# One start stage for the first block: load, norm and transpose by tiles of tokens, rotation table and first weights moved

## The chip, the cores and the metric

The kernel runs on one core of one Trainium2 chip. The metric is the time of one execution on the device in microseconds (us), smaller is better. The kernel is one launch of 42,208 instructions on five engines: TensorE (PE, matrix products; PEld is its weight load), VectorE (DVE), ScalarE (ACT), GpSimd (POOL) and SyncE (SP), which here issues nearly all DMAs. Each engine runs its own list of instructions in order. They meet at semaphores, and at a barrier of all engines at the end of each stage.

## The reference, cut to what matters

The program is two transformer-like blocks over 512 tokens of width 1024, all in float32. The change touches only the head of the first block: the load of `x`, the RMS norm, the transposed copy of the normed tokens, the cosine and sine tables for the rotation, and the beginning of the differential attention.

```python
y = xf * lax.rsqrt(jnp.mean(xf * xf, axis=-1, keepdims=True) + eps)
return (y * w.astype(jnp.float32)).astype(x.dtype)            # rms_norm, eps 1e-6
...
ang = positions.astype(jnp.float32)[..., None] * inv_freq
return jnp.cos(ang), jnp.sin(ang)                             # rotary_tables
...
return jnp.concatenate([t1 * c - t2 * sn, t2 * c + t1 * sn], axis=-1)   # apply_rotary on q and k
...
weights = probs[:, :, 0] - lam * probs[:, :, 1]               # diff_attention, lam from four vectors of 64
```

After the first block's attention come a state space scan, a mixture of 64 experts, two layers of a second block and a last norm. None of these is changed.

## The kernel before, in words

Every part is a stage: a function with the decorator `stage`, which ends with a barrier over all engines, so that the next stage's first instruction comes after the last of the stage before. Within a stage each engine has a hand-written list.

The start of the program is four stages. `stage_load` loads the table of constants (737.5 KB) and all of `x` (2048 KB) with two DMAs and waits for both. `stage_rope_tables` loads the positions, broadcast to 128 partitions, and makes two angle tables of 128x512 on VectorE (`RopeTable.angles`, lines 325 to 347): a cast and a multiplication by the frequencies, then for the cosine and for the sine a reduction of the angle to one turn. ScalarE then takes the two sines (`RopeTable.sines`). The position table lives in the buffer of the cosine, the table of turns in that of the sine. `stage_norm` squares the four tiles of 128 tokens on ScalarE (L401), takes one mean, one root (L405) and one reciprocal for all four, scales the rows on VectorE (L420), transposes them on TensorE in 8 groups of four 128x128 squares (L436), and splits each group into a rounded high part (ACT, L409, `h_hi`) and a remainder (DVE, L424, `h_lo`). All products with weights are made of three products of such parts.

`stage_attention` is a software pipeline over steps `u` from -7 to 35. Its weights are a `Stream` of tiles of 512 KB with three buffers each: SyncE loads a raw tile, ScalarE makes its high part (`make_hi`, L226), VectorE its low part (`make_lo`, L235), and TensorE may then start 24 matmuls with it (L284 to L286, `rows_of`). Each head has three tiles, for q, k and v, cut into four pieces of six rows of three matmuls. ScalarE takes a finished product to SBUF (`evacuate`, L604), TensorE turns its halves by a constant matrix (`half_turn`, L553), and VectorE multiplies by the cosine (L712) and the sine (L714) and adds (L718, in the function `rope`). The second `half_turn` waits until VectorE has read the first one's bank (`aux_roped`). Before the loop VectorE waits for five small DMAs, the four lambda vectors and a column of weights, before it makes the first low part:

```python
v.wait_ge(small_loaded, 80)
v.tensor_tensor(lam_prod[:], lam_rows[:, 0::2, :], lam_rows[:, 1::2, :], ALU.mult)
...
W.make_lo(v, 0)
W.make_lo(v, 1)
v.wait_ge(lam_exp, 1)
```

ScalarE makes two high parts, waits for VectorE's `dots_ready`, takes the exponentials of the lambdas, and enters the loop.

Of the kernel before, what the change touches and what calls it, by code (L numbers as in the profile page):

```python
# [291 lines left out]

@stage
def stage_load(k, x):
    nc = k.nc
    loaded = k.sem("start_loaded")
    with nc.Block() as block:
        @block.sync  # L300
        def _(sp):
            sp.dma_start(k.consts[:], k.const_dram[:, 0:FIRST_COLS]).then_inc(loaded, 16)
            sp.dma_start(k.x[:], x[0].rearrange("(t p) d -> p t d", p=P)).then_inc(loaded, 16)
            sp.wait_ge(loaded, 32)


class RopeTable:

    def __init__(self, k, ctx, tag, positions, freq, cos_out, sin_out):
        self.k, self.positions, self.freq, self.cos, self.sin = k, positions, freq, cos_out, sin_out  # L310
        self.pos_i = k.sb(f"{tag}_pos_i", [P, T], I32, ctx)
        self.pos_f, self.turns = cos_out, sin_out
        self.ang = k.sb(f"{tag}_ang", [P, 2, T], F32, ctx)
        self.pos_loaded, self.ang_ready = k.sem(f"{tag}_pos_loaded"), k.sem(f"{tag}_ang_ready")

    def load(self, sp):

# [1 line left out]

    def angles(self, v):  # L320

        two_pi = 2 * np.pi
# [5 lines left out]
        v.wait_ge(self.pos_loaded, 16)  # L328
        v.tensor_copy(pos[:], self.pos_i[:])
        v.drain()  # L330
        v.tensor_scalar(pos[:], pos[:], self.k.c(self.freq), None, ALU.mult)
        v.drain()
        for n, quarter in ((0, 0.25), (1, 0.0)):
# [15 lines left out]
    def sines(self, a):  # L349

        a.wait_ge(self.ang_ready, 2)
# [5 lines left out]
def stage_rope_tables(k, *table):  # L357

    with ExitStack() as ctx:
        rope = RopeTable(k, ctx, *table)  # L360
        with k.nc.Block() as block:
            @block.sync
            def _(sp):
                rope.load(sp)

            @block.vector
            def _(v):
                rope.angles(v)

            @block.scalar  # L370
            def _(a):
                rope.sines(a)


@stage
# [69 lines left out]


@stage
def stage_attention(k, W, lams, subln_w, att, merged, sig):

    nc = k.nc  # L450
    HEADS, UNITS, LEAD = 8, 32, 7
# [3 lines left out]
    with ExitStack() as ctx:  # L455
# [25 lines left out]
        with nc.Block() as block:  # L481
# [114 lines left out]
            def _(a):  # L596
# [64 lines left out]

                W.make_hi(a, 0)
                W.make_hi(a, 1)
                a.wait_ge(dots_ready, 1)
                a.activation(lam_dots[:], lam_dots[:], ACT.Exp).then_inc(lam_exp, 1)
                for u in range(FIRST, LAST):
                    if u + LEAD < UNITS + KD:
                        piece_before(u + LEAD)
                    if is_unit(u):
                        take_weights(u)  # L670
                    if is_unit(u + 2):
                        exps(u + 2)
                    if is_unit(u - 1):
                        take_out(u - 1)
                    if head_at(u, 5) is not None:
                        root(head_at(u, 5))
                    if head_at(u, 7) is not None:
                        out_hi(head_at(u, 7))
                    piece_after(u + LEAD)
                for m in range(KD):  # L680
                    W.make_hi(a, VALUES + 2 + m)

            @block.vector
            def _(v):
# [24 lines left out]
                def rope(n):  # L709
# [25 lines left out]
                def piece(g):  # L735
# [4 lines left out]
                    if part != 1:  # L740
                        W.make_lo(v, 3 * i + 2 + max(part - 1, 0))
                    if part >= 2:
                        rope(3 * i + part - 2)
# [9 lines left out]
                v.drain()  # L753
                v.tensor_scalar(lam_neg[:], lam_neg[:], -LAM_INIT, None, ALU.add)
                v.drain()
                for u in range(FIRST, LAST):
                    if is_unit(u + 2):
                        mask_and_max(u + 2)
# [7 lines left out]
                        out_lo(head_at(u, 7))  # L766
                    if u + LEAD < UNITS + KD:
                        piece(u + LEAD)
                for m in range(KD):
                    W.make_lo(v, VALUES + 2 + m)  # L770
                    v.wait_ge(W.used, VALUES + m + 1)
# [2730 lines left out]
def first_block(k, ap):  # L3502
# [4 lines left out]
    with ExitStack() as ctx:  # L3507
# [4 lines left out]
        with ExitStack() as h_ctx:  # L3512
            k.make_room_for_h("x", h_ctx, "right")
            with ExitStack() as att_ctx:
                k.make_room_for_rope("1", att_ctx)
                stage_rope_tables(k, "r1", ap["positions"], "freq64", k.cos, k.sin)
                stage_norm(k, "n1", ap["norm_mix_w"][0])
                stage_attention(k, W, [ap[n] for n in ("lambda_q1", "lambda_k1", "lambda_q2", "lambda_k2")], ap["subln_w"][0], k.x, merged, sig)
# [47 lines left out]
def build(nc, ap, consts, out):  # L3566
    with ExitStack() as ctx:
        k = Core(nc, ctx, consts)
        stage_load(k, ap["x"])
# [28 lines left out]
```

## Time and profile before

| | |
|---|---|
| median of 3 runs | 3816.51 us (3810.84 to 3816.89) |
| profiled execution | 3816.76 us, of which the span from first to last instruction is 3814.9 us |
| mean granted TensorE clock in the profiled execution | 0.923 of full speed |
| busy share of the span | PE 86%, PEld 61%, DVE 38%, ACT 29%, POOL 7% |
| first matmul of the attention stage | 54.05 us after the span's start |
| attention stage's first instruction | 42.15 us |

Busy time counts the work that an engine does. A timeline row says when an instruction starts, how long it runs, and how long the engine was idle before it and what ended that idle time. The table of slices gives the granted clock of TensorE, 1.00 for 2.4 GHz and 0.50 for 1.2 GHz.

### The profile page before, as it was taken

How to read it: one execution, taken by the hardware profiler on the slowest of the kernel's cores; microseconds unless marked ns; L12 is line 12 of the kernel's file. 1: busy time of each engine (PE TensorE's matmuls, PEld its weight loads, DVE VectorE, ACT ScalarE, POOL GpSimd, SP SyncE). 2: the span in 40 equal slices, each digit the busy share in tenths (PEclk: the TensorE clock that was granted, in tenths of full speed). 3: DMA queues.
4: the chain of work that ended last, by engine and by line, in shares of the span. 5: the costliest groups of instructions: out<-in, count | busy, mean ns of one | idle time of the engine just before them, and what ended most of it. 6: DMA issues, size and time to landing. Idle time of an engine off the chain costs nothing. (4 is left out here: it accounts for less than half of the span.)

```text
span 3814.9 us, 42208 instructions
## 1 busy us (share of the span) xinstructions
PE 3270.0 (86%) x16302; PEld 2316.5 (61%) x16302; DVE 1443.0 (38%) x2418; ACT 1111.4 (29%) x1899; POOL 269.3 (7%) x272
## 2 busy tenths in 40 slices
PE   4998999989588877887774978889998988969997
PEld 3776778778433333333333846768886846858886
DVE  4772466653420000000103555443323556353332
ACT  3672566652100000000002243232222244232221
POOL 0000222210000000000000001300000000400000
PEclk9999999999799999999996985989999986989999
DMA  3223222223599999999984200033323300023332
GB/s 95 61 67 64 78 56 67 67 62 116 217 417 426 426 426 425 423 422 412 418 339 136 66 12 4 1 94 95 98 96 85 83 12 4 1 78 94 97 97 77
DMA packets 355527, 601.99 MB, mean 158 GB/s; under 512 B 72288, under 2 KB 306560, under 8 KB 330624
## 3 DMA queue, kind: packets, MB, share of 16 engines
q1 hardware_dynamic: 346112, 590.85, 42.4%
q0 software_dynamic: 9216, 8.42, 0.7%
q8 instruction: 133, 2.18, 0.2%
q14 instruction: 66, 0.54, 0.0%
HBM read 603.40 MB, written 20.97 MB: 164 GB/s over the span
## 5 line engine op out<-in xcount | busy, mean ns | idle before, releaser
L1729 PE MATMUL ex_up<-ex_W,ex_XT 128*64 128x512 f32 x1024 | 256.9, 659 | 87.4 <-DMA ex_W<-in_w_expert_up_dram 87.4
L226 ACT ACTIVATE f_hi<-f_raw 128x1024 fp32r<-128x1024 f32 x148 | 156.8, 1059 | 565.6 <-PE ff_bk L286 550.0
L1729 PE MATMUL ex_gp<-ex_W,ex_XT 128*64 128x512 f32 x1024 | 246.4, 636 | 61.8 <-DMA ex_W<-in_w_expert_gate_dram 60.4
L235 DVE TENSOR_TENSOR f_lo<-f_raw,f_hi 128x1024 fp32r<-128x1024 f32 x148 | 181.1, 1224 | 257.4 <-ACT f_hi L226 257.2
L284 PE MATMUL ff_bk<-h_a_hi,f_hi 128*128 128x512 f32 x704 | 275.9, 392 | 2.8 <-DVE h_a_lo L3457 2.8
L285 PE MATMUL ff_bk<-h_a_lo,f_hi 128*128 128x512 f32 x704 | 275.4, 391 | 0.0
L286 PE MATMUL ff_bk<-h_a_hi,f_lo 128*128 128x512 f32 x704 | 275.3, 391 | 0.0
L1758 PE MATMUL ex_yp<-ex_W,ex_hT 128*64 128x512 f32 x1024 | 226.8, 594 | 37.0 <-DMA ex_W<-in_w_expert_down_dram 22.2
L1772 DVE TENSOR_TENSOR ex_hid<-ex_sg,ex_up 128x512 f32<-128x512 f32 x32 | 22.0, 688 | 610.7 <-PE ex_up L1729 610.7
L1729 PEld LDWEIGHTS ex_up<-ex_W,ex_XT 128*64 128x64 f32 x1024 | 93.0, 150 | 250.7 <-issue 250.7
L1729 PEld LDWEIGHTS ex_gp<-ex_W,ex_XT 128*64 128x64 f32 x1024 | 88.7, 146 | 218.6 <-issue 216.8
L235 DVE TENSOR_TENSOR b_lo<-b_raw,b_hi 128x1024 fp32r<-128x1024 f32 (+1 forms) x121 | 147.9, 1234 | 124.4 <-ACT b_hi L226 124.1
L284 PE MATMUL ff_bk<-f_hi,fT_hi 128*128 128x512 f32 x480 | 187.8, 391 | 0.0
L285 PE MATMUL ff_bk<-f_lo,fT_hi 128*128 128x512 f32 x480 | 187.5, 391 | 0.0
L286 PE MATMUL ff_bk<-f_hi,fT_lo 128*128 128x512 f32 x480 | 187.3, 390 | 0.0
L1758 PEld LDWEIGHTS ex_yp<-ex_W,ex_hT 128*64 128x64 f32 x1024 | 84.5, 137 | 157.2 <-issue 157.2
L284 PE MATMUL ss_acc<-h_x_hi,b_hi 128*128 128x512 f32 x320 | 132.6, 414 | 29.6 <-DVE b_lo L235 29.6
L226 ACT ACTIVATE b_hi<-b_raw 128x1024 fp32r<-128x1024 f32 (+1 forms) x121 | 125.7, 1048 | 110.0 <-PE mg_bk L286 64.9
L284 PEld LDWEIGHTS ff_bk<-h_a_hi,f_hi 128*128 128x128 f32 x704 | 133.2, 189 | 31.5 <-DVE h_a_lo L3457 3.6
L286 PEld LDWEIGHTS ff_bk<-h_a_hi,f_lo 128*128 128x128 f32 x704 | 133.1, 189 | 27.8
L285 PEld LDWEIGHTS ff_bk<-h_a_lo,f_hi 128*128 128x128 f32 x704 | 133.2, 189 | 27.5
L286 PE MATMUL ss_acc<-h_x_hi,b_lo 128*128 128x512 f32 x320 | 130.0, 406 | 0.0
(599 smaller groups left out, 6543.9 us busy)
## 6 DMA issues: line engine op xcount, KB each, us to landing
ex_W<-in_w_expert_gate_dram SPq DMA_DIRECT2D x64, 2048.0 KB, 28.8
ex_W<-in_w_expert_up_dram SPq DMA_DIRECT2D x64, 2048.0 KB, 29.1
ex_W<-in_w_expert_down_dram SPq DMA_DIRECT2D x64, 2048.0 KB, 28.9
b_raw<-in_w_in_dram SPq DMA_DIRECT2D x88, 512.0 KB, 3.9
f_raw<-in_w_gate_up_dram SPq DMA_DIRECT2D x88, 512.0 KB, 3.9
f_raw<-in_w_down_dram SPq DMA_DIRECT2D x44, 512.0 KB, 3.5
m_raw<-in_w_in_dram SPq DMA_DIRECT2D x40, 512.0 KB, 4.0
b_raw<-in_w_branch_ssd_dram SPq DMA_DIRECT2D x16, 512.0 KB, 4.0
```

Source lines behind the costliest of these rows:

```text
L226: a.activation(self.hi[n % self.SLOTS][:, at], self.raw[n % self.RAW][:, at], ACT.Copy).then_inc(self.cast, 1)
L235: v.tensor_tensor(self.lo[i][:, at], self.raw[n % self.RAW][:, at], self.hi[i][:, at].bitcast(F32), ALU.subtract).then_inc(self.split_done, 1)
L284: pe.matmul(out, a[0], b[0], start=first, stop=False)
L285: pe.matmul(out, a[0], b[1], start=False, stop=False)
L286: return pe.matmul(out, a[1], b[0], start=False, stop=last)
L1729: ins = pe.matmul(ps[part[e], :], XT[b][:, q, part[e]], row_view(slots[e], KD)[:, q, :], start=(q == 0), stop=(q == KD - 1))
L1758: ins = pe.matmul(y_ps[s][part[e], :], hT[:, q, part[e]], row_view(slots[e], HT)[:, q, s * 512:(s + 1) * 512], start=(q == 0), stop=(q == ...
L1772: v.tensor_tensor(hid[:], sg[:], u_ps[:], ALU.mult).then_inc(hid_ready, 1)
```

## The change

The load of `x`, the norm and the transposes become one stage, `stage_start`. SyncE loads the positions, tile 0 of `x`, the constants, the norm's weights, tiles 1 to 3 of `x` and then the first three tiles of the weight stream. Squares, means, roots, scaling, transposes and splits go by tiles of 128 tokens. VectorE makes the position table and the cosine's angles in this stage (`phases`, `reduce(v, (0,))`), after the mean of tile 0. The sine's angles are made in the attention stage, after the first two `make_lo`. The two sines and the exponentials of the lambdas are taken on ScalarE behind the first `evacuate`, in the loop. VectorE waits for the small DMAs after the sine's angles, and for the exponentials after its third step of the loop.

```diff
-@stage
-def stage_load(k, x):
...
+def stage_start(k, W, x, weight, rope):
...
             def _(sp):
                 rope.load(sp)
+                for t in range(NT):
+                    sp.dma_start(k.x[:, t, :], x[0, t * P:(t + 1) * P, :]).then_inc(x_loaded[t], 16)
+                    if t == 0:
+                        sp.dma_start(k.consts[:], k.const_dram[:, 0:FIRST_COLS]).then_inc(consts_loaded, 16)
+                        sp.dma_start(wbc[:], row_bc(weight)).then_inc(w_loaded, 16)
+                W.load_until(sp, W.RAW)
+
+            @block.scalar
+            def _(a):
+                for t in range(NT + 2):
+                    if t < NT:
+                        a.wait_ge(x_loaded[t], 16)
+                        a.activation(sq[:], k.x[:, t, :], ACT.Square, accum_out=ss[:, t:t + 1])
+                        a.drain().then_inc(ss_ready, 1)
+                    if 1 <= t <= NT:
+                        a.wait_ge(mean_ready, t)
+                        a.activation(ss[:, t - 1:t], ss[:, t - 1:t], ACT.Sqrt).then_inc(root_ready, 1)
+                    if t >= 2:
+                        for g in (2 * t - 4, 2 * t - 3):
+                            a.wait_ge(turned, g + 1)
+                            a.activation(part(k.h_hi, g), tiles(tp[g % 4]), ACT.Copy).then_inc(hi_ready, 1)
 
             @block.vector
             def _(v):
+                v.wait_ge(consts_loaded, 16)
+                rope.phases(v)
+                for t in range(NT + 2):
+                    if t < NT:
+                        v.wait_ge(ss_ready, t + 1)
+                        v.tensor_scalar(ss[:, t:t + 1], ss[:, t:t + 1], 1.0 / D, 1e-6, ALU.mult, ALU.add).then_inc(mean_ready, 1)
+                    if 1 <= t <= NT:
+                        n = t - 1
+                        v.wait_ge(root_ready, n + 1)
+                        v.reciprocal(ss[:, n:n + 1], ss[:, n:n + 1])
+                        v.drain()
+                        if n == 0:
+                            v.wait_ge(w_loaded, 16)
+                        v.scalar_tensor_tensor(h[:, n, :], k.x[:, n, :], ss[:, n:n + 1], wbc[:], ALU.mult, ALU.mult).then_inc(h_ready, 1)
+                    if t == 0:
+                        rope.reduce(v, (0,))
+                    if t >= 2:
+                        for g in (2 * t - 4, 2 * t - 3):
+                            v.wait_ge(hi_ready, g + 1)
+                            v.tensor_tensor(part(k.h_lo, g), tiles(tp[g % 4]), part(k.h_hi, g).bitcast(F32), ALU.subtract).then_inc(taken, 1)
...
 def stage_attention
                 W.make_hi(a, 0)
                 W.make_hi(a, 1)
-                a.wait_ge(dots_ready, 1)
-                a.activation(lam_dots[:], lam_dots[:], ACT.Exp).then_inc(lam_exp, 1)
...
                     piece_after(u + LEAD)
+                    if u == FIRST + 1:
+                        rope.sines(a, 1)
+                        a.wait_ge(dots_ready, 1)
+                        a.activation(lam_dots[:], lam_dots[:], ACT.Exp).then_inc(lam_exp, 1)
...
+                W.make_lo(v, 0)
+                W.make_lo(v, 1)
+                rope.reduce(v, (1,))
                 v.wait_ge(small_loaded, 80)
                 v.tensor_tensor(lam_prod[:], lam_rows[:, 0::2, :], lam_rows[:, 1::2, :], ALU.mult)
                 v.drain()
                 v.tensor_reduce(lam_dots[:], lam_prod[:], AX, ALU.add).then_inc(dots_ready, 1)
-                W.make_lo(v, 0)
-                W.make_lo(v, 1)
-                v.wait_ge(lam_exp, 1)
-                v.tensor_tensor(lam_neg[:], lam_dots[:, 1:2], lam_dots[:, 0:1], ALU.subtract)
...
+                    if u == FIRST + 2:
+                        v.wait_ge(lam_exp, 1)
+                        v.tensor_tensor(lam_neg[:], lam_dots[:, 1:2], lam_dots[:, 0:1], ALU.subtract)
```

TensorE's list in `stage_start` is that of `stage_norm`, behind a wait for the constants. `angles` still does both parts for the other two tables of the program.

## Rows read from the trace of the kernel before

**Rows 1.** The page, part 1: busy time and its share of the span
```profile
PE 3270.0 (86%) x16302; PEld 2316.5 (61%) x16302; DVE 1443.0 (38%) x2418; ACT 1111.4 (29%) x1899; POOL 269.3 (7%) x272
```

**Rows 2.** Timeline, load and table stages: start, length, engine, line, tiles, [idle <-releaser]
```profile
0.73 0.40 SPq L302 DMA_DIRECT2D consts<-in_shape_constants_dram  x1
1.19 0.42 SPq L303 DMA_DIRECT2D x_res<-in_x_dram  x1
...
14.23 0.43 DVE L329 CAST cos<-r_pos_i 128x512 f32<-128x512 int32 x1 [14.23 <-DMA r_pos_i<-in_positions_dram]
...
15.31 0.43 DVE L335 TENSOR_SCALAR sin<-cos 128x512 f32<-128x512 f32 x1
...
19.47 0.42 DVE L335 TENSOR_SCALAR sin<-cos 128x512 f32<-128x512 f32 x1
...
23.23 0.63 ACT L352 ACTIVATE cos<-r_ang 128x512 f32<-128x512 f32 x1 [10.75 <-DVE r_ang L347]
```

**Rows 3.** DMA issues in the first 60 us: KB each, median us from issue to landing
```profile
x_res<-in_x_dram SPq DMA_DIRECT2D x1, 2048.0 KB, 9.2
consts<-in_shape_constants_dram SPq DMA_DIRECT2D x1, 737.5 KB, 4.2
...
r_pos_i<-in_positions_dram SPq DMA_DIRECT2D x1, 256.0 KB, 3.0
```

**Rows 4.** Timeline, the norm's stage
```profile
25.05 1.06 ACT L401 ACTIVATE n_sq<-x_res 128x1024 f32<-128x1024 f32 x1 [0.67 <-PEq L134]
...
29.98 1.28 ACT L405 ACT_TABLE_LOAD   x1
31.27 0.20 ACT L405 ACTIVATE n_ss<-n_ss 128x4 f32<-128x4 f32 x1
...
31.78 4.87 DVE L420 SCALAR_TENSOR_TENSOR n_h<-x_res,n_ss,n_w 128x1024 f32<-128x1024 f32 x4
...
33.12 3.68 PE L436 MATMUL n_tp<-consts,n_h 128*128 128x128 f32 x16 [33.12 <-DVE n_h L420]
34.28 0.60 ACT L409 ACTIVATE h_x_hi<-n_tp 128x512 fp32r<-128x512 f32 x1 [2.80 <-PE n_tp L436]
35.13 0.60 ACT L409 ACTIVATE h_x_hi<-n_tp 128x512 fp32r<-128x512 f32 x1 [0.25 <-PE n_tp L436]
...
36.57 4.87 DVE L424 TENSOR_TENSOR h_x_lo<-n_tp,h_x_hi 128x512 fp32r<-128x512 f32 x8
```

**Rows 5.** Timeline, the attention stage's beginning
```profile
42.15 2.17 SPq L211 DMA_DIRECT2D b_raw<-in_w_in_dram  x3
...
46.14 1.06 ACT L226 ACTIVATE b_hi<-b_raw 128x1024 fp32r<-128x1024 f32 x1 [5.68 <-DMA b_raw<-in_w_in_dram]
...
52.20 0.29 DVE L746 TENSOR_TENSOR at_lam_prod<-at_lam_rows 128x128 f32<-128x128 f32 x1 [10.76 <-DMA at_wcol<-in_subln_w_dram]
...
52.78 2.35 DVE L235 TENSOR_TENSOR b_lo<-b_raw,b_hi 128x1024 fp32r<-128x1024 f32 x2
...
54.05 0.79 PE L284 MATMUL at_acc<-h_x_hi,b_hi 128*128 128x512 f32 x1 [14.22 <-DVE b_lo L235]
...
61.53 0.60 ACT L604 ACTIVATE at_plain<-at_acc 128x512 f32<-128x512 f32 x1 [7.48 <-PE at_acc L286]
...
63.10 1.23 DVE L235 TENSOR_TENSOR b_lo<-b_raw,b_hi 128x1024 fp32r<-128x1024 f32 x1 [6.35 <-ACT b_hi L226]
...
65.14 0.69 DVE L714 TENSOR_TENSOR at_turn<-at_aux,sin 128x512 f32<-128x512 f32 x1 [0.20 <-PE at_aux L553]
...
69.07 1.02 PE L553 MATMUL at_aux<-at_plain,consts 128*128 128x512 f32 x2
```

**Rows 6.** Windows: busy and count by engine, granted clock, DMA share, GB/s
```profile
54.00:56.00 2.00, 1.95 (x5) 1.57 (x6) 1.83 (x4) 0.05 (x1) 0.00 (x0) 0.50 0.32 64
...
58.00:60.00 2.00, 2.00 (x11) 1.62 (x10) 0.00 (x0) 0.00 (x0) 0.00 (x0) 1.00 1.16 304
...
100.00:200.00 100.00, 100.00 (x498) 73.75 (x496) 77.42 (x172) 62.78 (x165) 0.00 (x0) 1.00 0.21 59
```

More of the change, by code:

```diff
@@ L291, in row_bc @@
     return v.rearrange("(a n) -> a n", a=1).broadcast_to([n, v.shape[0]])
-@stage
-def stage_load(k, x):
[L297 to L304, printed above, removed]
 class RopeTable:
@@ L313, in __init__, with signals @@
         self.ang = k.sb(f"{tag}_ang", [P, 2, T], F32, ctx)
-        self.pos_loaded, self.ang_ready = k.sem(f"{tag}_pos_loaded"), k.sem(f"{tag}_ang_ready")
+        self.signals(tag)
+    def signals(self, tag):
+        self.pos_loaded, self.ang_ready = self.k.sem(f"{tag}_pos_loaded"), self.k.sem(f"{tag}_ang_ready")
     def load(self, sp):
@@ L320, in angles, with phases, reduce @@
     def angles(self, v):
+        self.phases(v)
+        self.reduce(v, (0, 1))
+    def phases(self, v):
+        pos = self.pos_f
+        v.wait_ge(self.pos_loaded, 16)
+        v.tensor_copy(pos[:], self.pos_i[:])
+        v.drain()
+        v.tensor_scalar(pos[:], pos[:], self.k.c(self.freq), None, ALU.mult)
+        v.drain()
+    def reduce(self, v, parts):
         two_pi = 2 * np.pi
@@ L327, in angles @@
         pos, turns = self.pos_f, self.turns
[L328 to L333, printed above, removed]
+        for n in parts:
+            quarter = (0.25, 0.0)[n]
             ang = self.ang[:, n, :]
@@ L347, in angles, with sines @@
             v.tensor_scalar(ang, ang, 3.1415925, -3.1415925, ALU.min, ALU.max).then_inc(self.ang_ready, 1)
-    def sines(self, a):
-        a.wait_ge(self.ang_ready, 2)
+    def sines(self, a, reduced=2):
+        a.wait_ge(self.ang_ready, reduced)
         a.activation(self.cos[:], self.ang[:, 0, :], ACT.Sin)
@@ L356, in stage_rope_tables @@
 @stage
-def stage_rope_tables(k, *table):
+def stage_start(k, W, x, weight, rope):
+    nc = k.nc
     with ExitStack() as ctx:
-        rope = RopeTable(k, ctx, *table)
-        with k.nc.Block() as block:
+        one = lambda n, s: k.sb("st_" + n, s, F32, ctx)
+        wbc, h, sq, ss = one("w", [P, D]), one("h", [P, NT, D]), one("sq", [P, D]), one("ss", [P, NT])
+        tp = k.banks(ctx, 4, "st_tp")
+        sem = lambda n: k.sem("st_" + n)
+        x_loaded, consts_loaded, w_loaded = [sem(f"x_loaded{t}") for t in range(NT)], sem("consts_loaded"), sem("w_loaded")
+        ss_ready, mean_ready, root_ready, h_ready, turned, hi_ready, taken = (sem(n) for n in ("ss", "mean", "root", "h_ready", "turned", "hi_ready", "taken"))
+        part = lambda x, g: x[:, (g % 2) * 4:(g % 2) * 4 + 4, (g // 2) * P:(g // 2 + 1) * P]
+        tiles = lambda bank: bank[:].rearrange("p (q n) -> p q n", q=4)
+        with nc.Block() as block:
             @block.sync
@@ L366, in _ @@
             @block.vector
             def _(v):
[L368 to L372, printed above, removed]
+                v.wait_ge(consts_loaded, 16)
[8 more added lines that the diff above has]
+                        v.reciprocal(ss[:, n:n + 1], ss[:, n:n + 1])
+                        v.drain()
+                        if n == 0:
[7 more added lines that the diff above has]
+                            v.tensor_tensor(part(k.h_lo, g), tiles(tp[g % 4]), part(k.h_hi, g).bitcast(F32), ALU.subtract).then_inc(taken, 1)
@@ new lines, in _ @@
+            @block.tensor
+            def _(pe):
+                pe.wait_ge(consts_loaded, 16)
+                for g in range(2 * NT):
+                    t = g // 2
+                    pe.wait_ge(h_ready, t + 1)
+                    if g >= 4:
+                        pe.wait_ge(taken, g - 3)
+                    for q in range(4):
+                        f = (g % 2) * 4 + q
+                        ins = pe.transpose(tp[g % 4][:, q * P:(q + 1) * P], h[:, t, f * P:(f + 1) * P], k.c("ident"))
+                    ins.then_inc(turned, 1)
@@ L447, in stage_attention @@
 @stage
-def stage_attention(k, W, lams, subln_w, att, merged, sig):
+def stage_attention(k, W, rope, lams, subln_w, att, merged, sig):
     nc = k.nc
@@ L742, in piece @@
                     if part >= 2:
-                        rope(3 * i + part - 2)
+                        turn_rows(3 * i + part - 2)
+                W.make_lo(v, 0)
+                W.make_lo(v, 1)
+                rope.reduce(v, (1,))
                 v.wait_ge(small_loaded, 80)
@@ L768, in _ @@
                         piece(u + LEAD)
+                    if u == FIRST + 2:
+                        v.wait_ge(lam_exp, 1)
+                        v.tensor_tensor(lam_neg[:], lam_dots[:, 1:2], lam_dots[:, 0:1], ALU.subtract)
+                        v.drain()
+                        v.tensor_scalar(lam_neg[:], lam_neg[:], -LAM_INIT, None, ALU.add)
+                        v.drain()
                 for m in range(KD):
@@ L3515, in first_block @@
                 k.make_room_for_rope("1", att_ctx)
-                stage_rope_tables(k, "r1", ap["positions"], "freq64", k.cos, k.sin)
-                stage_norm(k, "n1", ap["norm_mix_w"][0])
-                stage_attention(k, W, [ap[n] for n in ("lambda_q1", "lambda_k1", "lambda_q2", "lambda_k2")], ap["subln_w"][0], k.x, merged, sig)
+                rope = RopeTable(k, att_ctx, "r1", ap["positions"], "freq64", k.cos, k.sin)
+                stage_start(k, W, ap["x"], ap["norm_mix_w"][0], rope)
+                rope.signals("r1_rest")
+                stage_attention(k, W, rope, [ap[n] for n in ("lambda_q1", "lambda_k1", "lambda_q2", "lambda_k2")], ap["subln_w"][0], k.x, merged, sig)
             y = k.sb("ssd_y", [P, NT, 2 * D], F32, scan_ctx)
```

6 lines of the change are left out of this document (1 added, 5 removed).

## The prediction

> **What bounds the kernel now.** I read the page first. TensorE is busy for 86% of the span and no other engine for more than 38% [rows 1]. From the attention stage on it works nearly without a pause: the window from 100 to 200 us has 100.00 us of TensorE in 100 us, at the full clock [rows 6]. So the attention stage's end is set by when TensorE starts on it, as long as what feeds it keeps up. The second view was the timeline of the first 54 us, in which TensorE does 32 transposes of 128x128 and nothing else. There the chain is made of other things, one behind the other: the load of `x` and of the constants, the positions and the two angle tables, the two sines, four squares, one root, four scalings, eight transposed groups, a barrier, the weights' first tiles, and at last VectorE's wait for five small DMAs [rows 2 to 5]. The first attention matmul starts at 54.05 us [rows 5]. Stages end with a barrier and nothing after this one is tied to a fixed time of day, so what the first matmul wins, less what TensorE then loses by waits in the same stage, comes off the end. The chain of waits that the page follows back from the end does not reach this far, so I follow it.
>
> **The new start stage, DMA.** The consts' DMA is issued at 0.73 and lands 4.2 us later, at 4.9; `x` (2048 KB, 2.10 MB), issued at 1.19, lands 9.2 us later, at 10.4 [rows 2, 3]. So they go one after the other, `x` at 2.10 MB / 5.5 us = 381 GB/s. The 256 KB of positions take 3.0 us alone [rows 3], of which 0.26 MB / 381 GB/s = 0.7 is transfer and 2.3 latency. With seven DMAs queued from 0.73 on, and the latency paid once, the landings are: positions 3.7, `x` tile 0 (0.52 MB, 1.4 us) 5.1, constants (0.76 MB, 2.0) 7.1, norm weights 8.5, `x` tiles 1 to 3 at 9.8, 11.2 and 12.6. The three weight tiles follow (about 1.5 MB) and are there by some 18 us, well before they are used. Loading them costs the path nothing; the cover is the rest of this stage.
>
> **The new start stage, engines.** VectorE waits for the constants at 7.1. Cast and multiplication take 15.31 - 14.23 = 1.1 [rows 2]: 8.2. Mean of tile 0 (a tiny instruction, 0.2): 8.4. The cosine's angles 19.47 - 15.31 = 4.2 [rows 2]: 12.6. ScalarE has by then squared tile 0 and tile 1 (each 1.06 and 0.2 for its sum [rows 4]; tile 1 lands at 9.8, done 11.1) and taken the first root, even behind a table load of 1.28 [rows 4]: 12.6. VectorE: mean of tile 1, reciprocal, scaling of tile 0 (4.87 / 4 = 1.22 [rows 4]): h0 at 14.3. Here VectorE is what all wait for. From h0 on it must do three more scalings (3.7), eight low parts (4.87 [rows 4]) and a dozen tiny ones, 10 us or so with no wait. With the order as written: h1 is ready at 15.9; transposes of g0 are turned 34.28 - 33.0 = 1.3 after h0 and the next group 0.85 later [rows 4], high parts of g0 and g1 end at 16.2 and 17.0, low parts at 16.8 and 17.6. ScalarE squares tile 3 from 17.0 to 18.25, so the mean of tile 3 is at 18.4, h2 at 20.0, low parts of g2 and g3 at 21.2, h3 at 22.65. TensorE turns g6 by 23.9 and g7 by 24.75; the last high part ends at 25.35, the last low part at 25.95. The barrier costs 42.15 - 41.44 = 0.7 [rows 4, 5]. The attention stage starts at 26.65 in place of 42.15.
>
> **The attention stage, first matmul.** The weights are there, so ScalarE's first high part runs at once (1.06 [rows 5]), then VectorE's first low part, from whose start to the first matmul it is 54.05 - 52.78 = 1.27 [rows 5]. First matmul at 26.65 + 0.05 + 1.06 + 1.27 = 29.0. Gain: 25.0 us. Of it 15.5 are the start, and 9.5 the weights loaded earlier and the five small DMAs, which stood ahead of the first low part until 52.20 [rows 5].
>
> **What the attention stage pays.** On VectorE the second low part ends at 30.2, the sine's angles take 23.2 - 19.47 = 3.7 [rows 2]: 34.0. The small DMAs landed 52.20 - 42.15 = 10.05 after the stage's start, behind 2.17 us of issues for weights that are gone [rows 5]: between 34.5 and 36.7 now. Then 0.6 for the dots, and 1.2 for the third low part, 38.5 at the latest. TensorE wants that tile two rows before its second `half_turn`, 69.07 - 1.4 = 67.7, which is 42.7 with 25.0 taken off [rows 5]. No wait. On ScalarE the first `evacuate` comes at 61.53 - 25.0 = 36.5 [rows 5], and behind it a table load 1.28, two sines 1.15, a table load 1.28 and the exponential 0.2: 41.0. The fourth high part ends at 42.1 in place of 38.1, VectorE's fourth low part at 43.4. The first rotation is behind it; its product with the sine ended at 65.83, shifted 40.8 [rows 5], and now ends at about 44.6. The second `half_turn` waits for exactly that and would start at 69.07 - 25.0 = 44.05 [rows 5]. TensorE loses 0.6 us. The next pieces have slack again: the second evacuation is due at 42.9 and ScalarE is free by then, and TensorE needs the fourth tile only at about 49. If the small DMAs came 5 us later than my upper bound, the third low part would be the next to be late.
>
> **One rule weighed.** A table load takes 1.28, and the root after it starts 31.27 - 29.98 = 1.29 later, so nothing is added by the switch [rows 4]. The Trainium skill, "ScalarE: Activation LUTs", section "What ACT_TABLE_LOAD costs", adds a drain of about 1.38 us to each switch, and its rule is to batch functions of one set; this change puts the sine's and the exponential's set between two copies of the loop. By that figure the fourth high part would be 2.8 us later still and TensorE would lose 3.4 instead of 0.6. The trace disagrees, with 1.29 for load and start.
>
> **The clock.** At the first attention matmuls the granted clock is 0.50, the lower level of 1.2 GHz, with 5 matmuls in 2 us; from 58 us it is 1.00, with 11 [rows 6]. In between some eight matmuls took 0.425 us in place of 0.228, a price of 1.7 us. TensorE had been idle for 14.22 us then [rows 5], and will be for 29.0 - 24.75 = 4.3 us now, after transposes in pairs with gaps. Whether the clock is up or down at 29.0 the trace does not show. I take the same price as before, because both are starts after a pause; the bounds are 1.7 gained (never down) and 1.7 lost (down for twice as long).
>
> **Sum.** 25.0 - 0.6 = 24.4 us off. The profiled execution took 3816.76 (span 3814.9 and 1.9 around it), which is 0.2 above the median shown, so the forecast is 3816.6 - 24.4 = 3792 us. For the start stage I allow 2 us less (transposes at the full clock, fewer waits on VectorE: its work alone would end near 24) and 2.5 us more (a queue of seven DMAs slower than one, waits between the engines that I placed too kindly). The three runs before lie 6 us apart, which the median of the new runs can follow by 3 or so.
>
> **Rivals.**
> (a) A switch inside the loop costs twice its table load, because ScalarE must first run empty: 2 x 1.28 = 2.6 more [rows 4] in front of the fourth high part, and TensorE loses 3.2 instead of 0.6. Then 3792 + 2.6 = 3795. Against it stand the 1.29 us; chance 0.07.
> (b) The clock stays up over the short pause: 3792 - 1.7 = 3790; chance 0.13.
> (c) The change does not give the tiles early: the seven DMAs and the weights share the engines instead of going in order, and tile 0 comes with the last byte, at some 17.5. Then VectorE's positions are done by 18.6, h0 at about 24.7 in place of 14.3, and all is 10.4 later: 3802. Against it: consts landed at 4.9 while `x` was already queued and needed until 10.4 [rows 2, 3]. Chance 0.06.
> (d) Given back and more, by one mechanism: late feeding at the beginning of the attention makes TensorE stop and go, and the granted clock stays at 0.50 in the loop. Each 128x512 matmul then costs 0.2 us more; 24.4 us are gone after 122 of them, and the kernel is slower by over 0.2% after 160, that is if the low clock lasts from 29 to about 97 us: 3825. Against it: after the first 4 us the clock was 1.00 through the same pieces, and the one wait that I find is 0.6 us. Chance 0.02.
> (e) As (d) but cut short, or an unseen wait of some 20 us: within 0.2%; chance 0.02.
> My forecast itself has 0.70.
>
> **Numbers.** 0.2% is 7.6 us, about what the measurement can tell from no change; 3808.9 is the edge. Forecast, (a), (b) and (c) lie below it: 0.96 faster, 0.02 the same, 0.02 slower. The range from 3785 to 3799 holds forecast, (a) and (b) with the start stage's bounds and the runs' scatter, and leaves out (c) to (e).
>
> **What would show it.** The first instruction of the attention stage near 26.7 and its first matmul near 29.0. `h0` near 14.3, with VectorE the engine waited for between. Tile 0's square at about 5.1; if it starts after 9, (c) holds. The sines behind the first `evacuate`, 36.5 to 39.5, and the second `half_turn` with a wait under 1 us for the first rotation; if it waits 3, (a) holds. From there to the end every stage takes as long as before, within a few us. The prediction is wrong if the first matmul is early and the end is not, that is if a later stage grew, or if DMA landings are far later than in order.

## The result, and the profile after

| | before | changed |
|---|---|---|
| median, 6 runs each | 3813.68 us (3807.33 to 3819.52) | 3787.66 us (3786.62 to 3799.83) |
| profiled execution | 3816.76 us, span 3814.9 | 3786.62 us, span 3784.8 |
| attention stage's first instruction | 42.15 us | 28.06 us |
| its first matmul | 54.05 us | 30.45 us |
| its last matmul starts | 362.0 us | 338.4 us |

The ratio is 0.9937 with a 95% interval from 0.992 to 0.9953: 26.0 us off between the medians, where 24.4 were forecast (3792 us, from 3816.6 for the kernel before). The first matmul is 23.6 us earlier, and the last matmul of the attention stage 23.6 as well. The spans of the profiled executions differ by 30.1 us; the other 6.5 come much later, and the experiments turn to them.

The page of the changed kernel, part 1, answers to [rows 1]: the same work, in a shorter span.

```profile
PE 3269.9 (86%) x16302; PEld 2313.8 (61%) x16302; DVE 1444.8 (38%) x2424; ACT 1111.6 (29%) x1903; POOL 270.4 (7%) x272
```

The timeline of its start stage, which answers to [rows 2, 4]:

```profile
0.73 0.40 SPq L310 DMA_DIRECT2D r_pos_i<-in_positions_dram  x1
...
4.46 9.43 SPq L211 DMA_DIRECT2D b_raw<-in_w_in_dram  x3
6.53 1.06 ACT L387 ACTIVATE st_sq<-x_res 128x1024 f32<-128x1024 f32 x1 [4.52 <-DMA x_res<-in_x_dram]
...
8.36 0.43 DVE L321 CAST cos<-r_pos_i 128x512 f32<-128x512 int32 x1 [8.36 <-DMA consts<-in_shape_constants_dram]
...
11.36 1.06 ACT L387 ACTIVATE st_sq<-x_res 128x1024 f32<-128x1024 f32 x1 [3.68 <-DMA x_res<-in_x_dram]
...
12.59 1.28 ACT L391 ACT_TABLE_LOAD   x1
...
13.31 0.43 DVE L349 TENSOR_SCALAR r_ang<-r_ang 128x512 f32<-128x512 f32 x1
...
13.89 0.20 ACT L391 ACTIVATE st_ss<-st_ss 128x1 f32<-128x1 f32 x1
...
14.12 0.16 DVE L408 RECIPROCAL st_ss<-st_ss 128x1 f32<-128x1 f32 x1 [0.33 <-ACT st_ss L391]
14.37 1.28 DVE L412 SCALAR_TENSOR_TENSOR st_h<-x_res,st_ss,st_w 128x1024 f32<-128x1024 f32 x1
...
26.59 0.69 DVE L418 TENSOR_TENSOR h_x_lo<-st_tp,h_x_hi 128x512 fp32r<-128x512 f32 x1 [0.16 <-ACT h_x_hi L395]
```

Read the idle times: ScalarE waits for tile 0 until 6.53 and for tile 1 until 11.36, and only behind tile 1's square and a table load does it take tile 0's root, at 13.89. The first scaling starts at 14.37. VectorE had ended its angles at 13.74 and its second mean at 13.80 by then, and stood idle for 0.33 us until the root came.

The timeline of its attention stage, which answers to [rows 5]:

```profile
28.06 0.34 SPq L545 DMA_DIRECT2D at_lam_rows<-in_lambda_q_dram  x1
28.08 2.95 ACT L226 ACTIVATE b_hi<-b_raw 128x1024 fp32r<-128x1024 f32 x3 [1.52 <-PEq L134]
...
29.17 2.36 DVE L235 TENSOR_TENSOR b_lo<-b_raw,b_hi 128x1024 fp32r<-128x1024 f32 x2 [1.89 <-ACT b_hi L226]
...
30.45 0.79 PE L284 MATMUL at_acc<-h_x_hi,b_hi 128*128 128x512 f32 x1 [4.53 <-DVE b_lo L235]
...
37.72 0.60 ACT L663 ACTIVATE at_plain<-at_acc 128x512 f32<-128x512 f32 x1 [6.69 <-PE at_acc L286]
38.34 1.28 ACT L354 ACT_TABLE_LOAD   x1
...
43.27 1.23 DVE L235 TENSOR_TENSOR b_lo<-b_raw,b_hi 128x1024 fp32r<-128x1024 f32 x1 [5.80 <-ACT b_hi L226]
...
45.02 0.68 DVE L775 TENSOR_TENSOR at_turn<-at_aux,sin 128x512 f32<-128x512 f32 x1
...
45.84 1.10 PE L612 MATMUL at_aux<-at_plain,consts 128*128 128x512 f32 x2 [0.41 <-DVE at_turn L775]
```

The three high parts run at once, the first low part right behind, and TensorE waits 0.41 us at the second half turn for the product with the sine. The windows of the same kernel (columns as in [rows 6]) show the granted clock at 0.50 at the start of the matmuls and at 1.00 from 34 us on:

```profile
30.00:32.00 2.00, 1.55 (x4) 1.26 (x5) 1.92 (x4) 1.03 (x2) 0.00 (x0) 0.50 0.12 29
32.00:34.00 2.00, 2.00 (x7) 1.56 (x6) 1.76 (x3) 0.00 (x0) 0.00 (x0) 0.59 0.23 54
34.00:36.00 2.00, 2.00 (x11) 1.63 (x10) 1.41 (x3) 0.00 (x0) 0.00 (x0) 1.00 1.08 317
```

### The profile page after: what moved, and what is told of

The parts are those of the page before. It is cut to its first block and busy times, and to the rows that moved or that the text cites. A ratio compares the mean times of both kernels' runs of the same rounds, so it can differ in the third digit from the quotient of the medians.

```text
span 3784.8 us, 42176 instructions
## 1 busy us (share of the span) xinstructions
PE 3269.9 (86%) x16302; PEld 2313.8 (61%) x16302; DVE 1444.8 (38%) x2424; ACT 1111.6 (29%) x1903; POOL 270.4 (7%) x272
## 5 line engine op out<-in xcount | busy, mean ns | idle before, releaser
L1853 ACT ACTIVATE ex_hT<-ex_hp 128x512 f32<-128x512 f32 x32 | 19.1, 597 | 379.8 <-PE ex_hp L1810 379.8
```

The source lines that it names most:

```text
L1853: a.activation(hT[:].rearrange("p q n -> p (q n)"), h_ps[:], ACT.Copy).then_inc(ht_taken, 1)
```

## The experiments

### One part alone: preload, order, start stage

**Weights loaded in the norm's stage, nothing else** (on the kernel before):

```diff
-                stage_norm(k, "n1", ap["norm_mix_w"][0])
+                stage_norm(k, "n1", ap["norm_mix_w"][0], following=W)
```

> The kernel before, with the first three weight tiles loaded in the norm's stage and nothing else. My theory: the last wait before the first attention matmul is the five small DMAs, not the weights; they are issued 2.2 us earlier because no weight issues stand ahead of them, so the first matmul comes at 54.05 - 2.2 = 51.9 us. Rival (the preload is what pays): the whole landing time of the weights goes, and the first matmul comes at about 48.5 us or earlier.

Its timeline: the small DMAs are the last wait, as they were, and they end it 4.0 us earlier. The first of these rows is the issue of the last small DMA.

```profile
43.95 0.43 SPq L488 DMA_DIRECT2D at_wcol<-in_subln_w_dram  x1
...
48.17 0.29 DVE L746 TENSOR_TENSOR at_lam_prod<-at_lam_rows 128x128 f32<-128x128 f32 x1 [6.74 <-DMA at_wcol<-in_subln_w_dram]
...
50.02 0.79 PE L284 MATMUL at_acc<-h_x_hi,b_hi 128*128 128x512 f32 x1 [10.20 <-DVE b_lo L235]
```

The same issue in the kernel before:

```profile
47.37 0.43 SPq L488 DMA_DIRECT2D at_wcol<-in_subln_w_dram  x1
```

First matmul 50.02 us, where 51.9 and 48.5 had been expected. The wait that ended last was the one my theory names, but it ends 4.0 us earlier and not 2.2. Of the 4.0, 3.4 are the issues (47.37 - 43.95): no weight issues stand ahead of them, which is the 2.2, and the first small DMA's own issue takes 0.34 us in place of 1.53. The last small DMA then lands 4.2 us after its issue began, in place of 4.8.

**VectorE's order alone** (on the kernel before):

```diff
+                W.make_lo(v, 0)
+                W.make_lo(v, 1)
                 v.wait_ge(small_loaded, 80)
                 v.tensor_tensor(lam_prod[:], lam_rows[:, 0::2, :], lam_rows[:, 1::2, :], ALU.mult)
                 v.drain()
                 v.tensor_reduce(lam_dots[:], lam_prod[:], AX, ALU.add).then_inc(dots_ready, 1)
-                W.make_lo(v, 0)
-                W.make_lo(v, 1)
                 v.wait_ge(lam_exp, 1)
```

> The kernel before, with VectorE's first two low parts ahead of its wait for the small DMAs, weights still loaded in the attention stage. My theory: first matmul when the first weight tile has landed and its parts are made, 46.14 + 1.06 + 1.27 = 48.5 us, 5.6 earlier than before. ScalarE's third high part stays behind the exponential at about 53; TensorE wants that tile at about 61, so no new wait. Rival: the order is hidden, first matmul near 54.

```profile
47.21 1.23 DVE L235 TENSOR_TENSOR b_lo<-b_raw,b_hi 128x1024 fp32r<-128x1024 f32 x1 [5.67 <-ACT b_hi L226]
...
48.49 0.80 PE L284 MATMUL at_acc<-h_x_hi,b_hi 128*128 128x512 f32 x1 [8.56 <-DVE b_lo L235]
```

48.49 us, as expected to the tenth.

**Both together**, the two diffs above.

> Both of these edits together on the kernel before. My theory: first matmul at 42.15 + 0.05 + 1.06 + 1.27 = 44.5 us, 9.5 earlier, which is more than the sum of the two alone (2.2 + 5.6) because each hides the other's wait; the time falls by 9.5, ratio 0.9975. Rival (early starts are given back in the attention stage by late feeding): the first matmul at 44.5, but the stage's last matmul less than 7 us earlier.

```profile
44.78 0.80 PE L284 MATMUL at_acc<-h_x_hi,b_hi 128*128 128x512 f32 x1 [4.78 <-DVE b_lo L235]
```

First matmul 44.78 us, 9.3 earlier, and the last matmul of the stage at 351.8, 10.2 earlier: nothing is given back in this stage. Median 3807.65 us (10 runs) beside 3813.24 of the kernel before, 5.6 us off, ratio 0.9982 (0.9971 to 0.9992); 0.9975 was expected and is inside.

**The start stage alone**: the changed kernel's `stage_start` with the whole table in it, the sines at the end of ScalarE's list, no weights, and the attention stage in its old order.

```diff
-                W.load_until(sp, W.RAW)
...
-                        rope.reduce(v, (0,))
+                        rope.reduce(v, (0, 1))
...
+                rope.sines(a, 2)
```

> The other half: the new start stage with the whole rotation table and the sines in it, no weights loaded ahead, and the attention stage as before. My theory: the start stage is as long as VectorE's list, so the sine's angles add 3.7 us to the 27.3 us of the changed kernel and the sines some 2 more; attention starts near 33.5 and its first matmul is 11.9 later, near 45.4, 8.7 earlier than before; ratio 0.9977. Rival (the pipelined norm is the main gain, VectorE is not its bound): attention starts below 30 us and the first matmul comes below 42.

```profile
32.96 2.19 SPq L211 DMA_DIRECT2D b_raw<-in_w_in_dram  x3
...
43.03 0.29 DVE L805 TENSOR_TENSOR at_lam_prod<-at_lam_rows 128x128 f32<-128x128 f32 x1 [12.56 <-DMA at_wcol<-in_subln_w_dram]
...
44.88 0.80 PE L284 MATMUL at_acc<-h_x_hi,b_hi 128*128 128x512 f32 x1 [15.76 <-DVE b_lo L235]
```

The attention stage starts at 32.96 and its first matmul at 44.88, 9.2 earlier. Median 3804.8 us (10 runs), ratio 0.9971 (0.9961 to 0.9981). So the two halves give 9.3 and 9.2 of the 23.6; the last 5.1 are what the split of the table is for: the sine's angles and the two sines leave the start stage and lie under TensorE's first tile. A run below measures the angles' share as 3.6; the other 1.5 are the difference, and no run moves the sines alone.

### Taking one part out of the changed kernel

**No preload**: `W.load_until(sp, W.RAW)` removed from `stage_start`.

> The changed kernel with the three weight tiles loaded at the start of the attention stage again. My theory: they cost nothing where they are, because the queue serves the DMAs in order and they stand last; so the start stage is as long as in the changed kernel (attention stage from 28.1 us) and the first matmul waits for them, 4.0 us for landing as before, at about 34.4 us instead of 30.45. Rival (the weights share the engines with the tiles of x and slow them): the tiles of x are squared earlier than at 6.5 and 11.4 us, the start stage is 1 us or more shorter.

```profile
6.47 1.06 ACT L386 ACTIVATE st_sq<-x_res 128x1024 f32<-128x1024 f32 x1 [4.46 <-DMA x_res<-in_x_dram]
...
11.38 1.06 ACT L386 ACTIVATE st_sq<-x_res 128x1024 f32<-128x1024 f32 x1 [3.76 <-DMA x_res<-in_x_dram]
...
32.18 1.06 ACT L226 ACTIVATE b_hi<-b_raw 128x1024 fp32r<-128x1024 f32 x1 [5.61 <-DMA b_raw<-in_w_in_dram]
...
34.55 0.80 PE L284 MATMUL at_acc<-h_x_hi,b_hi 128*128 128x512 f32 x1 [8.62 <-DVE b_lo L235]
```

The two squares stand at 6.47 and 11.38 in place of 6.53 and 11.36: 1.5 MB queued behind the tiles of `x` do not delay them by anything that shows. The first matmul is 4.1 us later. The rival, that the weights share the engines with the tiles of `x` and slow them, falls.

**Positions third in the queue**:

```diff
-                rope.load(sp)
                 for t in range(NT):
...
                         sp.dma_start(k.consts[:], ...)
+                        rope.load(sp)
                         sp.dma_start(wbc[:], ...)
```

> The changed kernel with the broadcast of the positions moved behind tile 0 of x and the constants in the queue. Theory one (the queue needs its bytes in order and the broadcast at its head is slow to ramp up): tile 0 is squared at about 4.5 us instead of 6.5, and VectorE, which needs constants and positions, starts at about 8.0 instead of 8.4; first matmul 0.4 us earlier, 30.0. Theory two (seven DMAs in the queue share the engines): the square of tile 0 moves by less than 0.7 us.

```profile
4.05 1.06 ACT L387 ACTIVATE st_sq<-x_res 128x1024 f32<-128x1024 f32 x1 [2.04 <-DMA x_res<-in_x_dram]
...
8.11 0.43 DVE L321 CAST cos<-r_pos_i 128x512 f32<-128x512 int32 x1 [8.11 <-DMA r_pos_i<-in_positions_dram]
...
29.79 0.79 PE L284 MATMUL at_acc<-h_x_hi,b_hi 128*128 128x512 f32 x1 [4.53 <-DVE b_lo L235]
```

Tile 0 is there 2.5 us earlier, where 0.7 us of bytes had been reckoned for the positions: theory one holds as to the order of the queue. Its reason, a slow start at the queue's head, does not. The rate of all DMAs in steps of 0.25 us, first in this run from 0 to 10 us, then in the kernel before from 9 to 19 us, where the positions move alone:

```profile
GB/s 0 0 0 0 0 0 0 180 197 295 426 360 424 340 441 354 425 472 425 378 315 227 228 98 106 115 156 156 287 352 393 442 393 459 393 410 459 377 459 393
```

```profile
GB/s 475 344 115 16 0 0 0 0 0 0 0 0 49 172 205 188 148 172 107 8 0 0 0 0 0 0 0 0 0 0 0 0 0 0 0 0 0 0 0 0
```

In the middle of a full queue too the rate falls from above 400 GB/s to 98 to 156 when the positions are served, and they land 2.0 us after the constants (at 7.96 and 5.99). Alone they never pass 205 GB/s. So the broadcast moves slowly wherever it stands; why, no run here shows. The first matmul gains only 0.7, because ScalarE takes tile 0's root behind tile 1 anyway, and tile 1 is squared at 10.62 in place of 11.36.

**The whole table in the start stage**: `rope.reduce(v, (0, 1))` there, none in the attention stage, sines where the change has them.

> The changed kernel with the split of the rotation table undone: both parts of the angles on VectorE in the start stage, the sines still on ScalarE in the loop. My theory: VectorE is what the start stage waits for, so the stage is longer by the whole 3.7 us of the sine's angles: first matmul at about 34.2 us, and the 0.4 us that TensorE waits at the second half turn stays, because ScalarE's sines and exponential make it, not VectorE's angles. Rival (there is room on VectorE while it waits for tiles 1 to 3 of x): first matmul less than 2 us later.

The first matmul starts at 34.00 us, 3.6 later, and the last of the stage at 342.2, 3.8 later. TensorE's waits in the attention stage are the same, the 0.4 at the second half turn among them, which VectorE's angles therefore do not make. The angles' part of the split is worth 3.6 us, about the length that they have.

### What the start stage waits for

**The cosine's angles on GpSimd**: `phases` and the first part of the angles move to GpSimd in `stage_start`, each product-and-sum as two instructions.

```diff
-                rope.phases(v)
...
-                    if t == 0:
-                        rope.reduce(v, (0,))
...
+            @block.gpsimd
+            def _(g):
+                g.wait_ge(consts_loaded, 16)
+                rope.phases(g)
+                rope.reduce_cos_on_pool(g, tmp)
```

> The changed kernel with the position table and the cosine's angles on the idle GpSimd in the start stage, ten instructions more than on VectorE since its products and sums are apart. My theory: VectorE loses 5.3 us in front of the first scaling, which then waits for the norm's weights (landing near 10.1 us); the stage ends some 3.5 us earlier if GpSimd's list (12 instructions of about 1 us from 8.4 us on) is done by then: first matmul at about 27.0 us. Rival (GpSimd is the next bound, or slows VectorE): first matmul later than 29 us.

```profile
11.43 1.06 ACT L408 ACTIVATE st_sq<-x_res 128x1024 f32<-128x1024 f32 x1 [3.23 <-DMA x_res<-in_x_dram]
...
12.66 1.28 ACT L412 ACT_TABLE_LOAD   x1
...
14.19 0.16 DVE L427 RECIPROCAL st_ss<-st_ss 128x1 f32<-128x1 f32 x1 [1.41 <-ACT st_ss L412]
14.43 1.64 DVE L431 SCALAR_TENSOR_TENSOR st_h<-x_res,st_ss,st_w 128x1024 f32<-128x1024 f32 x1
...
16.28 2.10 DVE L431 SCALAR_TENSOR_TENSOR st_h<-x_res,st_ss,st_w 128x1024 f32<-128x1024 f32 x1
```

My theory fell. With VectorE free of 5.3 us of work the first scaling is no earlier (14.43 in place of 14.37), since VectorE waits 1.41 us for ScalarE's root, behind tile 1 and the table load. And beside a busy GpSimd VectorE's first three scalings take 1.64, 2.10 and 1.82 us, against 1.28 without; the fourth, which starts in a gap between two GpSimd instructions, takes 1.28. The first matmul came at 31.6 us, 1.2 later, so this run frees VectorE's list and slows VectorE at once, and does not tell what a free list alone is worth.

**Root behind its own square**, the root's table loaded at once by a root of a one, tile 0 scaled before the angles (VectorE's part is from `mean(0)` on), and the queue in the order tile 0, norm weights, constants, positions:

```diff
+                a.wait_ge(one_ready, 1)
+                a.activation(first[:], first[:], ACT.Sqrt)
+                square(0)
+                root(0)
+                high(0)
+                square(1)
+                root(1)
+                square(2)
...
+                mean(0)
+                v.wait_ge(w_loaded, 16)
+                scaled(0)
+                v.wait_ge(consts_loaded, 16)
+                rope.phases(v)
+                rope.reduce(v, (0,))
+                mean(1)
+                scaled(1)
```

> The changed kernel with another order in the start stage: the queue serves tile 0 of x, the norm's weights, the constants, the positions, then the rest; ScalarE loads the root's table at once with a root of a one, and takes each tile's root right behind its square, not behind the next tile's square; VectorE scales tile 0 before it makes the position table and the cosine's angles. My theory (in the changed kernel the first scaling waits for ScalarE behind tile 1's landing and a table load, as the run with GpSimd showed): tile 0 is scaled from about 7 us instead of 14.4, VectorE then has work without a gap, the stage ends some 3 us earlier and the first attention matmul comes near 27.4 us; time 3 us below the changed kernel's. Rival (VectorE's list alone sets the stage's end, so an earlier first scaling changes nothing): first matmul above 29.5 us.

```profile
6.52 1.28 DVE L425 SCALAR_TENSOR_TENSOR st_h<-x_res,st_ss,st_w 128x1024 f32<-128x1024 f32 x1
...
9.28 0.43 DVE L321 CAST cos<-r_pos_i 128x512 f32<-128x512 int32 x1 [1.48 <-DMA r_pos_i<-in_positions_dram]
...
15.18 1.29 DVE L425 SCALAR_TENSOR_TENSOR st_h<-x_res,st_ss,st_w 128x1024 f32<-128x1024 f32 x1
...
29.53 0.80 PE L284 MATMUL at_acc<-h_x_hi,b_hi 128*128 128x512 f32 x1 [4.52 <-DVE b_lo L235]
```

The first scaling is 7.9 us earlier and the first matmul 0.9: my forecast of 3 us fell, and the rival held (29.53, just above its 29.5). The run changes four things at once, and its 0.9 us is not divided among them. The second scaling, at 15.18 in place of 15.88, stands behind the angles, which wait for the positions until 9.28. So in the changed kernel two lists end within 0.33 us of each other: ScalarE's sets the first scaling, VectorE's stands close behind it, and freeing one leaves the other. Median 3791.28 us, ratio to the kernel before 0.9944 (0.9928 to 0.996): not to be told from the changed kernel by the times.

**The same, with the cosine's angles in the attention stage too**:

```diff
                 rope.phases(v)
-                rope.reduce(v, (0,))
...
-                rope.reduce(v, (1,))
+                rope.reduce(v, (0, 1))
...
-                        rope.sines(a, 1)
+                        rope.sines(a, 2)
```

> The last reordered kernel (root behind its own square, tile 0 scaled first), with the cosine's angles too moved into the attention stage; only the position table is made in the start stage. My theory: with its order freed, the start stage is as long as VectorE's list behind the landing of the positions, so 4.2 us of angles taken out of it shorten it by the 2.4 us until tile 1 of x becomes the limit: first matmul at about 27.1 us instead of 29.5. In the attention stage both angles are done at about 36.4, the third low part at 38.3 (due 40.7), the sines wait 0.6 us for them, and TensorE waits some 0.7 us at the second half turn instead of 0.4. Rival (the attention stage has no room for 4.2 us more on VectorE): TensorE waits over 2 us there and the stage's last matmul is no earlier than 338.4 us.

```profile
8.56 1.97 PE L459 MATMUL st_tp<-consts,st_h 128*128 128x128 f32 x8 [8.56 <-DMA consts<-in_shape_constants_dram]
...
12.92 1.29 DVE L425 SCALAR_TENSOR_TENSOR st_h<-x_res,st_ss,st_w 128x1024 f32<-128x1024 f32 x1
...
27.27 0.80 PE L284 MATMUL at_acc<-h_x_hi,b_hi 128*128 128x512 f32 x1 [4.52 <-DVE b_lo L235]
...
43.46 1.10 PE L641 MATMUL at_aux<-at_plain,consts 128*128 128x512 f32 x2 [0.43 <-DVE at_turn L804]
```

With both limits gone the second scaling starts at 12.92 and the first matmul at 27.27 us (27.1 expected), 3.2 earlier than in the changed kernel. The landing of tile 1, which was expected to be the next limit, is not: ScalarE squares it at 11.06 without an idle moment, straight behind tile 0's high parts, which wait for the transposes, and these for the constants until 8.56. TensorE waits 0.43 us at the second half turn, no more than before. The stage's last matmul starts at 336.5, 1.9 earlier than in the first profile of the changed kernel and 2.8 earlier than in its second. Part of the difference is the slow start of the matmuls: they follow each other at 0.43 us for ten steps here and for six in the first profile, so the first tile's product is taken 8.1 us after the first matmul in place of 7.3 (7.8 in the second profile). The granted clock does not show it this time, as the windows of this run give 1.00 there; the spacing of the matmuls does. Median 3786.59 us (6 runs), ratio 0.9924 (0.9911 to 0.9937) to the kernel before measured beside it. The changed kernel had 0.9937 and 0.9946 in its two measurements. So by the profile this is the better version; by the times it is likely, but the intervals overlap.

### The 6.5 us beyond the head

> The changed kernel as it is, beside the run of the same call with another order. First matmul at 30.4 us again. If the first profile's 6.5 us beyond the head are the change's doing, the first delta stage takes 118 us again, and the ratio to the kernel before is near 0.992. If they are the clock's chance, the stage may take 116 to 124 us, and the ratio is near 3790/3814 = 0.9938.

> The kernel before as it is. If the length of the first delta stage (123.7 us in the profile of before, 117.8 in that of the changed kernel) is chance, this profile may show either; if it is the change's doing, it shows 123.7.

In the first pair of profiles the first layer's delta stage (tiles `rc_*`) takes 123.7 us from its first to its last matmul before, and 117.8 after. Both kernels were profiled once more as they are. One window of 40 us from that stage's beginning, of the kernel before, of the same kernel again, and of the changed kernel; the column to read is the granted clock, the third number from the right, with TensorE's count of matmuls in the first bracket:

```profile
2348.00:2388.00 40.00, 37.75 (x244) 31.00 (x245) 19.33 (x47) 6.27 (x14) 16.15 (x13) 0.57 0.03 8
```

```profile
2349.00:2389.00 40.00, 36.44 (x290) 30.49 (x291) 22.00 (x51) 7.56 (x17) 18.08 (x14) 0.78 0.04 8
```

```profile
2323.00:2363.00 40.00, 34.31 (x294) 28.86 (x295) 22.44 (x51) 7.94 (x18) 18.09 (x14) 0.86 0.03 8
```

The kernel before, unchanged, does 290 matmuls there at a granted clock of 0.78 the second time, and 244 at 0.57 the first. Its stage takes 118.5 us in place of 123.7. The changed kernel again takes 118.6. The other kernels show 123.7 (both together), 124.3 (whole table), 123.8 (root first), 122.0 (no preload) and 115.8 to 119.4 (the rest), with no relation to how early they are. In the four profiles of 123.7 us or more the granted clock is 0.50 for the first 30 us of the stage, in the six of 117.9 or less for the first 10. So these 5.9 of the 6.5 us are a chance of the clock, and not of the change; why the clock rises sooner or later there stays open. The second pair of profiles agrees: their spans differ by 23.7 us (3809.7 and 3786.0), which is the head's gain alone.

The changed kernel's second measurement has 3793.29 us, ratio 0.9946 (0.9934 to 0.9959), 20.3 us below the 3813.54 beside it; the first had 26.0. Both intervals hold 0.9938, what the head's 23.6 us give. A single execution says little for the same reason: the preload alone and the order alone took 3802.80 and 3803.34 us, 10 us below the kernel before, with their first matmuls only 4.0 and 5.6 earlier and the delta stage at 116.0 and 115.9. The runs without a median above are therefore read by their rows and not by their times.

## Why the prediction was right

By its own steps:

- **The bound.** Right: what the first matmul wins comes off the end. 23.6 us at the first matmul, 23.6 at the stage's last, 23.3 at the first transposes of the stage behind the experts; beyond that the clock's chance adds its own.
- **DMA landings.** In order, as said, and the weights cost nothing. Mis-sized: tile 0 was used at 6.53 (forecast 5.1), the constants at 8.36 (7.1), tile 1 at 11.36 (9.8). The term that failed is the positions' 0.7 us of transfer at the rate of `x`. They landed 4.5 us after their issue at the head of the queue (3.0 alone), and took 2.0 us in its middle; the run with the positions third has tile 0 at 4.05. The split of the 3.0 us into 0.7 of transfer and 2.3 of latency was not read from any row, and the rate of the kernel before, above, speaks against it.
- **"Here VectorE is what all wait for."** Half wrong. I had the first root even with the angles, at 12.6; it ended at 14.09, and all of the 1.5 us is tile 1's late landing, since the table load stood in the forecast. The angles ended at 13.74 (12.6), 1.1 late with the constants. The first scaling began at 14.37 and ended near 15.65, forecast 14.3; ScalarE was the engine waited for there, by 0.33 us, and not VectorE. From the second tile on VectorE is close to the limit: taking its angles out of the reordered kernel gave 2.3 us. From the first scaling's end to the last low part it was 11.6 us, forecast 11.65; single low parts took 0.69 and pairs 1.28, a little more than the 4.87 / 8 = 0.61 that the forecast used, so part of that agreement is luck.
- **Start of the attention stage**: 28.06 us, forecast 26.65, 1.35 of the 1.4 from the two terms above. **First matmul**: 30.45, forecast 29.0, so 23.6 for 25.0.
- **The wait at the second half turn**: 0.41 us, forecast 0.6, at the place and for the reason given. The fourth high part started at 42.20, forecast 41.0 with the whole stage 1.4 later, so 0.2 sooner. The next pieces had slack.
- **The table loads in the loop**: from the load at 38.34 to the sine at 39.63 it is 1.29 us, and the load starts 0.02 us after the evacuation ahead of it ends. Rival (a) fell. The Trainium skill ("ScalarE: Activation LUTs", section "What ACT_TABLE_LOAD costs") adds about 1.38 us of drain to a switch; this trace disagrees, with those two numbers.
- **The clock**: 0.50 at the first matmul again, after a pause of 4.5 us in place of 14.2, and some seven slow matmuls in place of eight. Rival (b) fell. The price differed by 0.2 us in this pair of profiles (7.3 and 7.5 us to the first product); in the second pair the two kernels needed 7.8 and 8.1. The forecast's price of 1.7 us is 1.6 by its own numbers, 8 x (0.425 - 0.228); it was taken the same on both sides, so nothing hangs on it.
- **Sum**: the first matmul gained 23.6 (forecast 25.0), 0.4 went at the half turn (0.6) and 0.2 came back at the slow start: 23.4, where 24.4 were forecast, and the stage's last matmul shows 23.6. The time, 3787.7 for 3792.2, is off by 4.5 for other reasons: 2.9 since the kernel before had a median of 3813.68 in the comparison and not 3816.6, and 1.6 since the medians lie 26.0 apart. That 26.0, and the 20.3 of the second measurement, are scatter on both sides of 23.4; a forecast of 24.4 is nearer to the first of them by luck.

The rivals of a shared queue (c) and of a loop at the low clock (d) fell: the squares did not move with 1.5 MB taken away, the tiles landed in the order of the queue, and the granted clock was 1.00 in every window from 34 to 200 us. Tile 0's square, at 6.53, lay between the two signs given for it (5.1, and after 9 for (c)).

## What to carry to other kernels

A bound that is followed has to follow every engine's list: here the first scaling waited for ScalarE, which stood behind another tile's landing, while VectorE's work in the same stretch looked like the limit. Freeing ScalarE's order first gave 0.9 us, moving VectorE's angles to GpSimd lost 1.2 (with the slowing of VectorE in it), and freeing both gave 3.2. Small loads that nobody needs yet belong behind the first work that TensorE waits for, and they are cheap to find: look for the wait that ends last before TensorE's first instruction of a stage. Before putting microseconds down to a change, compare where along the kernel they appear; the delta stage of the unchanged kernel alone differed by 5.2 us between two profiles.

## What the runs showed of the hardware

- A broadcast of 256 KB (one row of 2 KB to 128 partitions) at the head of the queue delayed the tile behind it by 2.5 us (4.05 against 6.53), though it is only an eighth of the bytes that took 5.5 us in `x`. In the middle of the queue it took 2.0 us, at 98 to 156 GB/s where its neighbours moved at over 400.
- Three DMAs of 512 KB queued behind the others held SyncE's issue for 9.43 us (2.17 when issued into an empty queue [rows 5]), without delaying the tiles ahead of them.
- Three of VectorE's scalings of 128x1024 took 1.64 to 2.10 us while GpSimd worked on SBUF tiles, 1.28 without; the one that started in a gap between two GpSimd instructions took 1.28. GpSimd's instructions with a scalar on 128x512 ranged from 0.6 to 2.3 us in the same run.
- The same instructions of the first delta stage took 115.8 to 124.3 us over 14 profiles, by how long the granted clock stayed at 0.50 at its start.
- Matmuls followed each other at 0.43 us in a window whose granted clock was given as 1.00 (27 to 31 us in the last reordered kernel); the spacing is the surer sign of the two.
